# Rotary embedding's row exchange by four small transfers, and eight norms' rows from one product

## The reference

```python
def rmsnorm(x, g):
    return x * rsqrt(mean(x * x, axis=-1) + EPS) * g
def layernorm(x, g, b):
    mu = mean(x); xc = x - mu
    return xc * rsqrt(mean(xc * xc) + EPS) * g + b
def partial_rope(t, cos, sin):          # t: one head of 64; half = 8
    t1, t2 = t[..., :8], t[..., 8:16]
    return concat([t1 * cos - t2 * sin, t2 * cos + t1 * sin, t[..., 16:]])
# block 1
x = x + 0.5 * swiglu(rmsnorm(x))                     # norm f1
z = rmsnorm(x) @ w_in                                # norm mix; z -> q, k, v, conv inputs, gates
q, k = partial_rope(rmsnorm_head(q)), partial_rope(rmsnorm_head(k))
a = sliding_window_attention(q, k, v, sinks) @ attn_proj
u = depthwise_conv31(ca * sigmoid(cb))
c = silu(layernorm(u)) @ conv_proj                   # norms ln_mu, ln_r
x = x + (sigmoid(ga) * a + sigmoid(gb) * c) @ w_out
x = x + 0.5 * swiglu(rmsnorm(x))                     # norm f2
e = rmsnorm(p @ ple_proj)                            # norm e
x = x + sigmoid(rmsnorm(x) @ ple_gate_w) * e         # norm gate
# block 2
proj = rmsnorm(x) @ w_in_2                           # norm mix2
...                                                  # pooling, delta rule, cross-attention
x = x + sqrelu_mlp(rmsnorm(x))                       # norm f3
return rmsnorm(x)
```

## Time and profile before

| | |
|---|---|
| median of 3 runs | 2023.91 us (2018.24, 2023.91, 2024.28) |
| the profiled execution | 2018.09 us, span 2016.3 us |
| PE busy | 1985.0 us, 98% |
| DVE busy, ACT busy | 1210.0 us (60%), 809.3 us (40%) |
| granted TensorE clock | 0.997 |

### The profile page before, as it was taken

How to read it: one execution, slowest core, us unless ns; L and a number is a source line. 1 busy time by engine, 2 the same in 40 slices (tenths; PEclk the granted TensorE clock), 3 DMA queues, 4 the chain that set the end, 5 groups by cost and what they waited for, 6 DMA issues and landing times. The chain is left out here.

```text
span 2016.3 us, 26767 instructions
## 1 busy us (share of the span) xinstructions
PE 1985.0 (98%) x10554; PEld 1631.9 (81%) x10554; DVE 1210.0 (60%) x1714; ACT 809.3 (40%) x1232; POOL 16.2 (1%) x31
## 2 busy tenths in 40 slices
PE   8999999999999999999999999999999999999998
PEld 6888888887677788888888888877888888888887
DVE  6666565687889545654434367886464456544544
ACT  5444443433777253523322245541354432222222
POOL 0000000000000000000000000010000000000000
PEclk9999999999999999999999999999999999999999
DMA  6999886454333453333333233211143322223221
GB/s 238 300 301 294 291 292 238 173 177 141 120 116 121 172 188 111 110 103 95 94 97 96 88 101 94 84 43 35 38 135 117 109 90 94 94 95 105 94 95 72
DMA packets 80347, 274.84 MB, mean 136 GB/s; under 512 B 8928, under 2 KB 11488, under 8 KB 80224
## 3 DMA queue, kind: packets, MB, share of 16 engines
q1 hardware_dynamic: 79648, 272.36, 41.2%
q10 hardware_dynamic: 576, 0.79, 0.1%
HBM read 240.61 MB, written 32.51 MB: 135 GB/s over the span
## 5 line engine op out<-in xcount | busy, mean ns | idle before, releaser
L340 PE MATMUL ps<-Hh,whi 128*128 128x512 f32 x1448 | 571.8, 395 | 11.6 <-DVE Hl L1785 8.2
L344 PE MATMUL ps<-Hh,wlo 128*128 128x512 f32 x1448 | 564.6, 390 | 0.0
L341 PE MATMUL ps<-Hl,whi 128*128 128x512 f32 x1448 | 564.3, 390 | 0.0
L1098 ACT CAST whi<-raw 128x1024 fp32r<-128x1024 f32 (+3 forms) x352 | 350.0, 999 | 362.7 <-PE ps L344 339.8
L1757 DVE TENSOR_TENSOR wlo<-raw,whi 128x1024 fp32r<-128x1024 f32 (+3 forms) x294 | 338.4, 1157 | 171.0 <-ACT whi L1098 166.4
L340 PEld LDWEIGHTS ps<-Hh,whi 128*128 128x128 f32 x1448 | 272.3, 188 | 74.8 <-issue 12.8
L341 PEld LDWEIGHTS ps<-Hl,whi 128*128 128x128 f32 x1448 | 272.4, 188 | 57.0 <-issue 1.9
L344 PEld LDWEIGHTS ps<-Hh,wlo 128*128 128x128 f32 x1448 | 272.3, 188 | 57.1
L1873 DVE SCALAR_TENSOR_TENSOR cacc<-upad,gains,cacc 128x512 f32<-128x512 f32 x232 | 160.0, 743 | 0.7
L1823 DVE SCALAR_TENSOR_TENSOR x<-ps,x 128x512 f32<-128x512 f32 x79 | 54.6, 691 | 152.8 <-PE ps L344 152.8
L1799 DVE TENSOR_TENSOR scr<-ps,Rt 128x512 f32<-128x512 f32 x92 | 63.0, 686 | 56.5 <-PE ps L344 34.1
(11 more groups left out here) (379 smaller groups left out, 2788.6 us busy)
## 6 DMA issues: line engine op xcount, KB each, us to landing
raw<-in_w SPq DMA_DIRECT2D x369, 512.0 KB, 4.1
low_parts<-lo SPq DMA_DIRECT2D x58, 512.0 KB, 4.4
wlo<-low_parts SPq DMA_DIRECT2D x58, 512.0 KB, 3.5
raw<-in_w SPq DMA_DIRECT2D x16, 384.0 KB, 3.1
raw<-in_w SPq DMA_DIRECT2D x17, 256.0 KB, 2.6
out<-y SPq DMA_DIRECT2D x8, 256.0 KB, 2.0
x<-in_x SPq DMA_DIRECT2D x5, 256.0 KB, 6.6
raw<-in_w SPq DMA_DIRECT2D x8, 128.0 KB, 2.0
```

The source lines that it names most:

```text
L340: e.matmul(out, h[:, kk, :], a, start=part != "last" and k + kk == 0, stop=False)
L341: e.matmul(out, h[:, kk, :], c, start=False, stop=False)
L344: ins = e.matmul(out, lo[:, kk, :], a, start=False, stop=done)
L1098: e.copy(whi[i % WS][:, 0:n], raw[i % RAWS][:, 0:n]).then_inc(*act.tick("whi", ("whi", i)))
```

## The change

The permutation product and its wait go from PE. In their place ACT issues four transfers per tile, of 8 partitions each, from `g` to the other 8 rows of a second buffer (scr[5] for even tiles, cleared once by POOL at the start, and scr[2] for odd ones). The other rows of these buffers meet zeros in `ropeS`. DVE waits for the four transfers where it waited for the permutation.

For eight norms (f1, ln_mu, ln_r, f2, e, gate, mix2, f3) the four column products, the square root, the reciprocal and the four spreading products become one product of a column of 1/1024, broadcast, by `acc` (`mean_row`); ACT then takes Ln in place in the bank and Exp with scale -0.5, into `Rt` (`norm_row`) or in place (`root_row`); ln_mu needs neither. Norms mix, xq, mem, the delta rule's and the last keep the old way.

```diff
-            glob = np.zeros((128, 260), np.float32)
+    glob[:, 260] = 1.0 / D
...
@@ build
+        turned_g = (scr[5], scr[2])
...
@@ tensor_program
+            def mean_row(key, *up, src=acc, c=260, n=T, pin=False):
+                b = take(("R", key), pin)
+                pe.wait_ge("ld", "cg")
+                pe.wait_ge(*up)
+                e.matmul(b[:, 0:n], cg[:, c:c + 1].to_broadcast([128, 128]), src[:, 0:n], start=True, stop=True).then_inc(*pe.tick("spread", ("spread", key)))
+            def norm_row(name):
+                mean_row(name, "sum", name, 7)
...
-            ffn("f1", ..., [nothing, lambda: norm_columns("f1"), lambda: norm_R("f1")])
+            ffn("f1", ..., [nothing, lambda: norm_row("f1")])
...
                 ins.then_inc(*pe.tick("sums", ("rope_ss", tile)))
-                b2 = take(("perm", tile))
-                pe.wait_ge("rope_g", tile)
-                e.matmul(b2[:, :], perm, g[:, :], start=True, stop=True).then_inc(*pe.tick("perm", ("perm", tile)))
...
                 if j == 3:
-                    take(("cols", "ln"))
-                    pe.wait_ge("conv_sum")
-                    columns("ln", acc, ps(("cols", "ln")))
+                    mean_row("ln_mu", "conv_sum", pin=True)
                 if j == 7:
-                    b = take(("cols", "lnv"))
-                    pe.wait_ge("sum", "lnv", 7)
-                    columns("lnv", acc, b)
+                    ring.append(bank_of["R", "ln_mu"])
+                    mean_row("ln_r", "sum", "lnv", 7, pin=True)
             for j in range(3, 8):
                 gate_b(j)
-                if j == 3:
-                    spread("ln_r", cols(("r", "lnv"), 4), ("r", "lnv"))
+            ring.append(bank_of["R", "ln_r"])
...
                 gemm(("pl", j), "ple_proj", 0, 2, [(128 * j, 128)], ph, pl, "p")
                 if j == 2:
-                    norm_columns("f2")
-                if j == 4:
-                    norm_R("f2")
+                    norm_row("f2")
...
@@ scalar_program
+            def norm_row(name, prev, n=T):
+                b = ps(("R", name))[:, 0:n]
+                act.wait_ge("spread", name)
+                e.activation(b, b, AF.Ln, bias=epsc, scale=1.0).then_inc(*act.tick("sd", ("ln", name)))
+                act.wait_ge("ln", name)
+                if prev:
+                    act.wait_ge("R_done", prev)
+                e.activation(Rt[:, 0:n], b, AF.Exp, scale=-0.5).then_inc(*act.tick("R", ("R", name), ("free", ("R", name))))
...
                 e.activation(g[:, :], ps(("rope", tile))[:, :], AF.Copy, scale=gcol("q_norm" if tile else "k_norm")).then_inc(
                     *act.tick("rope_g", ("rope_g", tile), ("free", ("rope", tile))))
+                if tile == 0:
+                    act.wait_ge("turned0")
+                if tile == 1:
+                    act.wait_ge("vt")
+                act.wait_ge("rope_g", tile)
+                for i, to in enumerate((0, 8, 64, 72)):
+                    at_ = to + (8 if i % 2 == 0 else -8)
+                    e.dma_start(turned_g[tile % 2][to:to + 8, :], g[at_:at_ + 8, :]).then_inc(*act.tick(f"swap{tile % 2}", ("swap", tile, i), by=16))
...
             for j in range(8):
                 after(("pl", j))
                 if j == 3:
-                    deviation("f2", 4, 1.0 / D)
-                if j == 5:
-                    norm_R("f2", "mix")
+                    norm_row("f2", "mix")
...
@@ vector_program
             def rope(tile):
-                g, r = scr[tile % 2], scr[2]
+                g, r = scr[tile % 2], turned_g[tile % 2]
-                dve.wait_ge("perm", tile)
-                ...
-                e.tensor_tensor(r[:, :], ropeS, ps(("perm", tile))[:, :], MUL).then_inc(...)
+                dve.wait_ge("swap", tile, 3)
+                e.tensor_tensor(r[:, :], ropeS, r[:, :], MUL).then_inc(*dve.tick("rope", ("rope_r", tile)))
...
-                dve.wait_ge("spread", "ln_r")
+                dve.wait_ge("R", "ln_r")
...
@@ pool_program
+            e.memset(scr[5][:, :], 0.0).then_inc(*pool.tick("zero", ("turned0",)))
```

More of the change, by code:

```diff
@@ L434, in tensor_program @@
             ssq, ssk = take("ssq", pin=True), take("ssk", pin=True)
-            pe.wait_ge("ld", "c1")
             def rope_stats(tile):
-                s, g = scr[3 + tile % 2], scr[tile % 2]
+                s = scr[3 + tile % 2]
                 pe.wait_ge("rope_sq", tile)
@@ L567, in tensor_program @@
                 if j == 2:
-                    norm_columns("f2")
-                if j == 4:
-                    norm_R("f2")
-            def e_columns():
-                b = take(("cols", "e"))
-                pe.wait_ge("sum", "e", 7)
-                columns("e", acc, b)
-            ffn("f2", "f2", Hh, Hl, "ffn2_wgu", "ffn2_wdown", True, [nothing, nothing, e_columns, nothing, lambda: spread("e", cols(("r", "e"), 4), ("r", "e"), pin=True)]
-                + [nothing] * 9 + [lambda: ring.append(bank_of["R", "e"])])
+                    norm_row("f2")
+            ffn("f2", "f2", Hh, Hl, "ffn2_wgu", "ffn2_wdown", True, [nothing, nothing, lambda: mean_row("e", "sum", "e", 7, pin=True)]
+                + [nothing] * 11 + [lambda: ring.append(bank_of["R", "e"])])
             for j in range(8):
@@ L584, in tensor_program @@
                 if j == 0:
-                    norm_columns("gate")
-                if j == 1:
-                    norm_R("gate")
+                    norm_row("gate")
             def conv4(i):
@@ L604, in tensor_program @@
             c5(range(7))
-            norm_columns("mix2")
+            norm_row("mix2")
             c4((7,))
             c5((7,))
-            c6 = begun(("cv", 6), "w_in_2", 1280, Hh, Hl, "mix2")
-            c6(range(4))
-            norm_R("mix2")
-            c6(range(4, 8))
+            conv4(6)
             conv4(7)
@@ L1131, in deviation, with root_row @@
                     *act.tick("sd", ("sd", key), ("free", ("cols", frees[0] if frees else key))))
+            def root_row(key, scale=1.0):
+                b = ps(("R", key))[:, :]
+                act.wait_ge("spread", key)
+                e.activation(b, b, AF.Ln, bias=epsc, scale=scale).then_inc(*act.tick("sd", ("ln", key)))
+                act.wait_ge("ln", key)
+                e.activation(b, b, AF.Exp, scale=-0.5).then_inc(*act.tick("R", ("R", key)))
+            def norm_row(name, prev, n=T):
[6 more added lines that the diff above has]
+                e.activation(Rt[:, 0:n], b, AF.Exp, scale=-0.5).then_inc(*act.tick("R", ("R", name), ("free", ("R", name))))
             def norm_R(name, prev, n=T):
@@ L1339, in scalar_program @@
                 if j == 3:
-                    deviation("lnv", 4, 1.0 / D)
+                    root_row("ln_r")
                 for i in range(3 * j - 12, min(3 * j - 9, 8)) if j > 3 else ():
@@ L1358, in scalar_program @@
                     act.wait_ge("gemm", ("gb", 7))
-                    act.wait_ge("cols", "lnv")
+                    act.wait_ge("spread", "ln_r")
                 norm_tile("f2", "ffn2_norm", j, x[:, j, :], Hh)
@@ L1377, in glu_e @@
                 if f == 1:
[L1378 removed]
+                    root_row("e")
                 glu(tag, f)
@@ L1413, in scalar_program @@
                 if j == 1:
-                    deviation("gate", 4, 1.0 / D)
-                    norm_R("gate", "f2")
+                    norm_row("gate", "f2")
                     gate_sig(0)
@@ L1444, in scalar_program @@
             after(("cv", 4))
-            deviation("mix2", 4, 1.0 / D)
+            norm_row("mix2", "gate")
             after(("cv", 5))
-            norm_R("mix2", "gate")
             after(("cv", 6))
@@ L1837, in vector_program @@
             weights(4)
-            reciprocal("f1", 4)
             for what, b in ffn_order("f1"):
@@ L2166, in vector_program @@
             after(("pg", 0))
-            reciprocal("gate", 4)
             after(("pg", 1))
@@ L2217, in vector_program @@
             after(("cv", 4))
-            reciprocal("mix2", 4)
             after(("cv", 5))
@@ L2608, in vector_program @@
                     after(("f3", "u", f))
-                    if f == 0:
-                        reciprocal("f3", 4)
                     sqrelu(f)
```

50 lines of the change are left out of this document (14 added, 36 removed).

## The result

| | before | after |
|---|---|---|
| median | 2023.35 us (4 runs, 2018.24 to 2024.28) | 1999.56 us (4 runs, 1998.93 to 2002.88) |
| the profiled execution, span | 2016.3 us | 2001.0 us |

The ratio is 0.990, with a 95% interval of 0.9885 to 0.9916: the kernel is about 1.0% faster.

What follows compares the result with a forecast made beforehand. PE, busy 1985.0 of 2016.3 us, was taken as the bound. Terms 7.7 + 7.5 + 0.9 + 1.4 - 1.7 = 15.8 us off 2018.09 or 2023.91 gave 2002.3 or 2008.1; forecast 2006, range 1998 to 2014.

Steps and rivals of the forecast that it cites:

- Permutation: Rotation: removing nine permutation products from PE, 0.86 us each, saves 7.7 us.
- Norms: Eight norms on PE: one row product replaces column and spreading products, saving 0.94 us each, 7.5 us in all.
- ln_r's wait: Before ln_r's spreading products: PE's wait for a reciprocal queued on DVE goes, saving 0.9 us.
- The wait for the squares' sum: At ln_r: PE's wait of 1.5 us for the sum of squares stays, since the new product needs it too.
- Head start of DVE: Rotation's end into softmax: head norm starts 3.2 us earlier, DVE gains 1.4 us on PE, and 1.4 us of waits go.
- One sign: Rotation tiles in the new profile: DVE's wait is for DMA and under 2 us.
- f2: Projection of p and feed-forward: ACT's longer chain makes PE wait 0.8 and 0.85 us, costing 1.7 us; bounds 0 and 2.5.
- The second: Feed-forward behind f2: PE waits 0.85 us for g1's low part, after SP's load of u0 slips.
- rival 1: Rotation to convolution's end: DVE stays the bound, PE loses 7.6 us at conv_sum; gain only 8.2 us, chance 0.10.
- rival 2: ACT's new norms: one table load serves Ln and Exp, f2's 1.7 us is not lost; gain 17.5 us, chance 0.06.
- rival 3: Rotation: turned rows land late; gain 10.9 us at 7.5 us landing, 6 us slower at 11; chance 0.06.
- rival 4: Whole kernel: change does not show on PE, through row product cost or waits at other norms; gain about 4 us, chance 0.10.

Runs made afterwards that it cites:

- rotation_only: The changed kernel with all eight norms put back the old way, keeping the four transfers per tile; 2009.29 us, ratio 0.9943 to the kernel before.
- norms_only: The changed kernel with the permutation product back in place of the transfers, keeping the eight new norms; 2010.44 us, ratio 0.9953 to the kernel before.
- split_swaps: The changed kernel with two of each tile's four transfers issued from POOL's queue instead of ACT's; 2002.61 us, ratio 0.9915 to the kernel before.
- again: The changed kernel measured once more without any edit; 2002.56 us, ratio 0.9907 to the kernel before.
- Six_swaps: The changed kernel with two more transfers per tile issued ahead of the four; 2005.11 us, ratio 0.9927 to the kernel before.
- f2_late: The changed kernel with ACT's Ln and Exp of norm f2 moved behind the casts for pl 6 and pl 7; 2004.85 us, single run, no ratio.
- double_swap: The changed kernel with eight transfers per tile instead of four, the added ones into rows meeting zeros; 2016.04 us, ratio 0.9976 to the kernel before.
- g_first: The changed kernel with ACT's square of the tile moved behind g and the four transfers; 2001.73 us, ratio 0.9906 to the kernel before.

## Why the prediction was right

The range, 1998 to 2014, held the time, and the forecast of 2006 was 6.4 us too high. The mechanism was right: PE's stream got shorter by the work that left it, and DVE let it. By the landmarks the change is worth 17.4 us (16.40 at G and f3's 0.98), 1.6 more than the sum of 15.8. The rest of the 6.4 is the level of the runs. The prediction subtracted 15.8 us from two levels, 2018.09 and 2023.91, and settled between. From the lower one its sum gives 2002.3; the profiled execution took 2002.88, and the other three 1998.93 to 1999.91. From the median it gives 2008.1, which is 8.5 too high. Before has medians between 2019.7 and 2023.4 in the four measurements. Which level the four runs would hit could not be known, so that the range held the time is in part luck; what bears the prediction out are the landmarks, term by term.

1. **Permutation, 7.7 us.** Right: 7.64 from A to B in the change, in its repetition and in rotation_only, 0.01 in norms_only. It was read from the starts of PE, as 9 times 0.86, and not from durations, which overlap.
2. **Norms, 0.94 each.** Right: the row product costs 0.855, and gate, mix2 and f3 gave 0.97, 0.96 and 0.98. The first, f1's, lies ahead of A (1.02 with the program's start offset by 0.25 us).
3. **ln_r's wait, 0.9.** Right: it is gone, and rotation_only still has it. C to D holds ln_mu, ln_r and this wait, 3.07 us, 0.3 more than the 2.8 counted; norms_only shows the same 3.07. The 0.3 are the wait, which the prediction read from the idle time in brackets and not from starts. Around the row there stand in the kernel before:

```profile
704.80 0.39 PE L344 MATMUL ps<-Hh,wlo 128*128 128x512 f32 x1
...
707.30 0.39 PE L341 MATMUL ps<-Hl,whi 128*128 128x512 f32 x1
```

   That is 2.50 us, less 0.455 for two plain rows and 0.895 for the spreading products: the wait cost 1.15 us. The wait for the squares' sum stayed at 1.5 us, as said:

```profile
687.38 1.10 PE L392 MATMUL ps<-acc,cg 128*128 128x512 f32 x2 [1.54 <-DVE acc L1784]
```

4. **Head start of DVE, 1.4.** Right in size, by luck: two errors cancel. ACT and then DVE around tile 8, after the change:

```profile
478.98 0.68 ACT L1225 ACTIVATE scr<-ps,gains 128x512 f32<-128x512 f32 x1
479.69 2.96 ACTq L1234 DMA_DIRECT2D scr<-scr  x4
```

```profile
484.04 0.69 DVE L1928 TENSOR_TENSOR scr<-c,scr 128x512 f32<-128x512 f32 x1 [1.19 <-DMA scr<-scr]
...
485.97 0.21 DVE L1936 TENSOR_TENSOR rq<-small,ps 128x64 f32<-128x64 f32 x1
```

   An issue takes 0.63 us on ACT, not the 0.47 of the earlier trace rows, and the last of tile 8 starts 0.3 us late besides: the four take 2.96 us, where the prediction had 1.9. From their end, 482.65, to DVE it is 1.4 us, where it had 2.6. From the end of g, 479.66, to DVE that makes 4.4 us; the prediction had 4.7. The head norm starts 7.49 us behind tile 8's square (478.48), where it had started 10.89 behind it: 3.4 earlier against 3.2 predicted. Counted from the last issue's start, 482.0, DVE goes on 2.0 us later, and 2.0 to 2.2 us in the five tiles in which it waits for the transfers. The Trainium skill (DMA: Bandwidth & Descriptors, the section on one DMA's anatomy) gives a fixed part of about 2.0 us, for transfers that GpSimd issues. ACT's transfers in this trace agree with it, though they take another queue; GpSimd's own, 3.3 us in split_swaps, don't. The waits for P fell from 4.7 to 3.3, the amount said; the other two profiles with the same transfers and taps have 3.5 (`again`) and 3.1 (rotation_only). Six_swaps confirms the slope: 1.3 us later, 1.3 to 1.5 us lost. One sign was off: DVE's wait for the transfers was to be under 2 us in each tile, and in the first it is 3.1.

5. **f2, -1.7.** This is the term that was mis-sized: it cost 0.7, and that is 1.0 of the 1.6 us that the sum was short. ACT, then PE:

```profile
808.49 1.28 ACT L1130 ACT_TABLE_LOAD   x1
809.78 0.66 ACT L1130 ACTIVATE ps<-ps,cg 128x512 f32<-128x512 f32 x1
810.46 1.28 ACT L1134 ACT_TABLE_LOAD   x1
811.76 0.60 ACT L1134 ACTIVATE Rt<-ps 128x512 f32<-128x512 f32 x1
812.25 1.65 ACT L1084 CAST whi<-raw 128x256 fp32r<-128x256 f32 x3
816.79 1.05 ACT L1084 CAST whi<-raw 128x1024 fp32r<-128x1024 f32 x1 [2.89 <-DMA raw<-in_w]
```

```profile
811.86 0.39 PE L346 MATMUL ps<-ph,wlo 128*128 128x512 f32 x1
812.79 0.47 PE L342 MATMUL ps<-ph,whi 128*128 128x512 f32 x1 [0.54 <-ACT whi L1084]
```

   The first wait is there, 812.79 - 811.86 - 0.23 = 0.70, predicted 0.8: pl 6's cast stands behind Ln, the load and Exp. The second, 0.85 for g1's low part, is not. The 4.6 us for SP's load of u0 were taken from the profile of before as if a transfer had a fixed time; here its cast starts at 816.79, 3.6 us after the low part that frees the buffer. The chain had 0.85 us at stake and the transfer alone moved by 1.0. D to E gives 1.15 us: two norms of 0.94 less 0.7. In the profiles of the other kernels with the same norms it is 0.85 to 1.18, f2_late apart.

6. **DVE not the bound** (rival 1). Right. DVE ends the convolution 1.5 us before PE wants it, as in the earlier trace rows; DVE first, then PE:

```profile
660.80 0.69 DVE L1884 TENSOR_TENSOR acc<-acc,upad 128x512 f32<-128x512 f32 x1
663.02 1.02 PE L392 MATMUL ps<-acc,cg 128*128 128x512 f32 x2
```

7. **One load for Ln and Exp** (rival 2). Wrong for this kernel: two loads of 1.28 us stand around each Ln, at 808.49 and 810.46 above. The Trainium skill (ScalarE: Activation LUTs, the section on table sets) counts one load for ln followed by exp; the rows show two, and the measurement decides. How many there are is settled when the program is built; by the prediction's own sum a kernel built with one would not lose the 0.7 us of f2. That was not tried.

8. **Slower, by late rows** (rival 3). The transfers landed in 2.0 us and the rival had no ground here, but double_swap shows that such a turn exists, only at another place than the one named. The rival had the way of a buffer from DVE back to ACT as the bound. What becomes the bound is ACT itself, when 8 issues of 0.65 make its tile 7.45 us long against PE's 6.35. Four issues leave 1.3 us of ACT more than six do, and six still fit.

9. **Does not show on PE** (rival 4). It had no ground: each norm that could be read singly gave 0.96 to 0.98 us, and from 700 us to G PE has no wait but f2's.

What stays open: why the two P waits of 1.5 and 1.3 us don't react to anything tried. In that part of the softmax ACT reloads its table before and after a gate of the convolution (L1202, L1269), 1.28 us each; that these loads cause the waits was not tested.

## What to carry to other kernels

When PE is busy 98% of the time, price what leaves it from the starts of the rows around it, and a product that PE doesn't need is worth exactly that; four issues on ScalarE's queue were a cheap substitute because its tile of work, issues included, stayed shorter than PE's. Add up the tile of the engine that takes over the work before you trust its mean load: at 41% busy, six issues a tile still fitted and eight made it the bound. A PE that is made to wait can lose more than the wait: in double_swap and f2_late its clock halved right behind. When a term hangs on a transfer's time that you read once, give it the spread of that time, and when runs of before lie on two levels, say which one the sum starts from.

## What the runs showed of the hardware

- An issue of a 16 KB transfer of 8 rows from SBUF to SBUF holds ScalarE for 0.63 us, against 0.47 for the loads at the start, and GpSimd for 0.53. From the last issue's start to the waiting VectorE instruction it took 2.0 to 2.2 us in the changed kernel and 2.6 in tile 8 of g_first; a transfer issued by GpSimd landed 3.3 us after its issue. None of it counts as busy time in the page.
- One fp32 product of 512 columns, two records, costs 0.855 us on PE, nearly four times a plain row of 0.23.
- Stretches of 3.4 or 6.8 us with the granted clock at 0.50 occur in the middle of a program that keeps PE busy 98% of the time; one of 3.4 us cost 1.6 us. Among other places they were seen at 1388 and 1429 us (before), 1291, 1380 and 1414 (after), 1293, 1382 and 1416 (again), 1368 and 1412 (g_first), 477, 518 and 1382 (double_swap) and 818, 1371 and 1415 (f2_late), and between the start and the last norm there is none in rotation_only and norms_only. Ahead of them PE had waited (1.2 us or more at 477, 518 and 818) or made narrow products (4x4 at 1291). What brings them about was not tried.
- At the start of every profile PE's first rows, from 8 us on, also follow each other at 0.43 us, until 11 to 14 us; the view of windows gives a granted clock of 1.00 there, so it is read from the rows alone.
